# Attention scores of two heads issued together, with the low-part products on the two halves of the array

## What is computed

```python
def stick_breaking_attention(q, k, v):
    """q, k, v: (B, H, S, Dh). A[t,s] = beta_ts * prod_{s<j<t}(1 - beta_tj), strictly causal."""
    for start in range(0, S, SB_BLOCK):          # SB_BLOCK = 128 queries
        end = start + SB_BLOCK
        z = jnp.einsum('bhqd,bhkd->bhqk', qb, kb) * scale
        log_keep = jnp.where(valid, jax.nn.log_sigmoid(-z), 0.0)
        later = lax.cumsum(log_keep, axis=3, reverse=True) - log_keep
        w = jnp.where(valid, jnp.exp(jax.nn.log_sigmoid(z) + later), 0.0)
        outs.append(jnp.einsum('bhqk,bhkd->bhqd', w, vb))
```

## Time and profile before

| | |
|---|---|
| runs of before | 958.69 us median, 957.64 to 959.88 |
| profiled execution | 959.37 us, of it 957.4 us span |
| attention stage on PE | from 179.67 us (load of the first scores) to about 312 us |
| busy over the span | PE 932.1, PEld 783.3, DVE 515.2, ACT 325.8, POOL 215.9 us |
| granted PE clock | full but for a few short stretches |

### The profile page before, as it was taken

One profiled execution on the slowest core, in us unless ns is written; L12 is line 12 of the kernel. 1 busy time (PEld: TensorE's weight loads), 2 busy tenths in 40 slices (PEclk: granted clock), 3 DMA queues, 4 the chain that ended last, 5 costly groups with the idle time before them and its releaser, 6 DMA issues.

```text
span 957.4 us, 13833 instructions
## 1 busy us (share of the span) xinstructions
PE 932.1 (97%) x5547; PEld 783.3 (82%) x5547; DVE 515.2 (54%) x769; ACT 325.8 (34%) x740; POOL 215.9 (23%) x130
## 2 busy tenths in 40 slices
PE   6999999999999999999999999999999899999998
PEld 6788889778877888888888888888888678888886
DVE  4976899698986355444043183133336753334322
ACT  7852122487876221212811100223224720120000
POOL 0003414520010122222243222101110236762000
PEclk9999999999999999999999999999999999999999
DMA  9942503510211211111222536211117574435321
GB/s 315 296 146 71 150 2 110 157 35 25 58 48 42 66 52 44 44 44 56 78 77 90 153 100 172 83 45 55 46 51 251 185 240 106 153 115 180 106 88 66
DMA packets 122697, 100.55 MB, mean 105 GB/s; under 512 B 18087, under 2 KB 104704, under 8 KB 122378
## 3 DMA queue, kind: packets, MB, share of 16 engines
q1 hardware_dynamic: 92330, 76.07, 26.4%
q10 hardware_dynamic: 30304, 23.60, 8.1%
HBM read 73.44 MB, written 24.12 MB: 102 GB/s over the span
## 4 chain that ended last, share of the span: by engine, by line
PE 80%; DVE 11%; ACT 3%; DMA 2%; issue 2%; POOL 0%; SPq 0%; POOLq 0%; ACTq 0%; DVEq 0%
PE psum L845 48%; PE psum L272 5%; PE psum L274 5%; PE psum L273 5%; PE psum L281 4%; PE psum L1093 3%; DVE gacc L544 2%; DVE sq L720 2%; PE psum L1062 2%; PE psum L1430 1%; DMA adag<-in_ada_w 1%; PE psum L1064 1%; DVE ss L722 1%; DVE rows L732 1%; PE psum L1524 1%
## 5 line engine op out<-in xcount | busy, mean ns | idle before, releaser
L845 PE MATMUL psum<-hhi,w3hl 128*128 128x512 f32 x1120 | 368.3, 398 | 5.3 <-POOL w3hl L834 3.3
L845 PEld LDWEIGHTS psum<-hhi,w3hl 128*128 128x128 f32 x1120 | 211.0, 188 | 49.8 <-issue 6.5
L845 PE MATMUL psum<-hlo,w3hl 128*128 128x512 f32 x560 | 219.0, 391 | 0.0
L834 POOL TENSOR_TENSOR w3hl<-w3raw,w3hl 128x1024 fp32r<-128x1024 f32 x43 | 104.8, 2436 | 456.5 <-DVE w3hl L827 456.5
L845 PEld LDWEIGHTS psum<-hlo,w3hl 128*128 128x128 f32 x560 | 105.7, 189 | 19.7
L1192 DVE TENSOR_TENSOR_SCAN stick<-stick,floor 128x1024 f32<-128x1024 f32 (+7 forms) x64 | 89.3, 1441 | 14.4 <-ACT stick L1140 14.1
L845 PE MATMUL psum<-ohi,w3hl 128*128 128x512 f32 x256 | 79.0, 389 | 0.0
L929 ACT COPY zst<-psum 128x512 f32<-128x512 f32 x44 | 25.9, 588 | 131.4 <-PE psum L845 128.0
L680 PE MATMUL psum<-w,hhi 128*128 128x512 f32 x192 | 67.7, 397 | 0.6 <-ACT rows L704 0.6
L827 DVE CAST w3hl<-w3raw 128x1024 fp32r<-128x1024 f32 x43 | 29.5, 686 | 66.6 <-DMA w3raw<-in_w_in 36.7
L845 PEld LDWEIGHTS psum<-ohi,w3hl 128*128 128x128 f32 x256 | 48.0, 188 | 9.9
(11 more groups left out here) (228 smaller groups left out, 1556.2 us busy)
## 6 DMA issues: line engine op xcount, KB each, us to landing
z_scratch<-zst ACTq DMA_DIRECT2D x44, 256.0 KB, 2.3
w3raw<-in_w_in ACTq DMA_DIRECT2D x20, 512.0 KB, 4.2
ada<-in_ada_w SPq DMA_DIRECT2D x16, 512.0 KB, 7.5
w3raw<-in_w_in SPq DMA_DIRECT2D x16, 512.0 KB, 4.0
sg<-z_scratch SPq DMA_DIRECT2D x8, 1024.0 KB, 7.3
xrow<-in_x SPq DMA_DIRECT2D x4, 1024.0 KB, 6.1
w1raw<-in_w_in SPq DMA_DIRECT2D x4, 1024.0 KB, 7.1
adag<-in_ada_w SPq DMA_DIRECT2D x8, 512.0 KB, 4.0
```

Of the source, the lines that this page charges most:

```text
L834: nc.gpsimd.tensor_tensor(lo, w3raw[:], cast(hi), ALU.subtract).then_inc(w3_lo, 1)
L845: t = nc.tensor.matmul(out_, a[:, kt, :], moving[b][:, kt, 512 * half:512 * half + 512], start=(ends[0] and kt == k0 and m == 0), stop=(en ...
```

## The change

- `scores` runs at even steps only and makes the scores of both heads (steps n and n + 1): first the 128-row products of head 0 and head 1 (L1064 of the changed file), then the products with the keys' low parts (L1069), each over 64 rows: head 0 on partitions 0 to 63, head 1 on 64 to 127, the heads alternating, each into its own bank.
- Its wait on `keep_ok` is now for n, that is for the sigmoids of steps n - 2 and n - 1. At the first step of a pair it waits for all four `low` parts and all duplicates, where before the fourth `low` part was awaited by the second head alone.
- The high part of head 1 and the low parts are stored on the head's own partitions (`own_rows`); the duplicate of the keys goes out as two DMAs of 64x512 instead of one of 64x2x512.
- The zeros in `qk` part 2 and their two memsets on POOL, with the waits on them, are gone.

```diff
--- before.py
+++ after.py
@@ -994,6 +994,10 @@
         def o_cols(m):
             return bank(7)[:, P * (m % 2):P * (m % 2) + P]
 
+        def own_rows(head):
+
+            return slice(HD * head, HD * head + HD)
+
         def half_of(u):
 
             part, half = TURNS[u % 4]
@@ -1005,7 +1009,9 @@
 
                 pp, _, cols = half_of(u)
                 sp.wait_ge(fh_ok, u + 1)
-                sp.dma_start(cast(qk[HD:P, pp, 1, :, cols]), cast(qk[0:HD, pp, 1, :, cols])).then_inc(dup_ok, 16)
+                for head in range(2):
+                    a, b = own_rows(head), own_rows(1 - head)
+                    sp.dma_start(cast(qk[b, pp, 1, head, cols]), cast(qk[a, pp, 1, head, cols])).then_inc(dup_ok, 16)
 
             for u in range(2):
                 second_half(u)
@@ -1045,25 +1051,27 @@
                 f.then_inc(q_mm, 1)
 
             def scores(n):
-                pair, qb, head = steps[n]
-                if n == PER:
-                    pe.wait_ge(c2_ok, 3)
+
+                pair, qb, _ = steps[n]
                 if n % PER == 0:
-                    pe.wait_ge(fl_ok, 4 * pair + 3)
-                    pe.wait_ge(dup_ok, 32 * (pair + 1))
-                if n % PER == 1:
                     pe.wait_ge(fl_ok, 4 * pair + 4)
+                    pe.wait_ge(dup_ok, 64 * (pair + 1))
                 if n >= 2:
-                    pe.wait_ge(keep_ok, n - 1)
-                q, k_hi, k_lo = (qk[:, pair % 2, i, head] for i in range(3))
-                for c0 in range(0, keys(n), 512):
-                    c1 = min(c0 + 512, keys(n))
-                    z = bank(2 * (n % 2) + c0 // 512)
-                    nc.tensor.matmul(z[:, 0:c1 - c0], q[:, P * qb:P * qb + P], k_hi[:, c0:c1], start=True,
-                                     stop=False, skip_group_check=True)
-                    m = nc.tensor.matmul(z[:, 0:c1 - c0], q[:, P * qb:P * qb + P], k_lo[:, c0:c1], start=False,
-                                         stop=True, skip_group_check=True)
-                m.then_inc(z_mm, 1)
+                    pe.wait_ge(keep_ok, n)
+                parts = [(c0, min(c0 + 512, keys(n))) for c0 in range(0, keys(n), 512)]
+                for head in range(2):
+                    for c0, c1 in parts:
+                        nc.tensor.matmul(bank(2 * head + c0 // 512)[:, 0:c1 - c0],
+                                         qk[:, pair % 2, 0, head, P * qb:P * qb + P],
+                                         qk[:, pair % 2, 1, head, c0:c1], start=True, stop=False, skip_group_check=True)
+                for c0, c1 in parts:
+                    for head in range(2):
+                        m = nc.tensor.matmul(bank(2 * head + c0 // 512)[:, 0:c1 - c0],
+                                             qk[own_rows(head), pair % 2, 0, head, P * qb:P * qb + P],
+                                             qk[own_rows(head), pair % 2, 2, head, c0:c1], start=False, stop=True,
+                                             skip_group_check=True)
+                        if c1 == keys(n):
+                            m.then_inc(z_mm, 1)
 
             def flips(n):
 
@@ -1101,9 +1109,7 @@
             for u in range(4):
                 turn(u)
             fill_2(pe, -1)
-            pe.wait_ge(c2_ok, 1)
             scores(0)
-            scores(1)
             for n in range(NST + 5):
                 if n == 2:
                     pe.wait_ge(e_in, 16)
@@ -1111,7 +1117,7 @@
                         t = nc.tensor.transpose(bank(7)[:, ST * pair:ST * pair + ST], vE[:, P * pair:P * pair + P],
                                                 ident[0:ST, 0:ST])
                     t.then_inc(ve_mm, 1)
-                if n + 2 < NST:
+                if n % 2 == 0 and n + 2 < NST:
                     scores(n + 2)
                 fill_2(pe, n)
                 if turn_at(n) is not None:
@@ -1130,7 +1136,7 @@
                 if u == 4:
                     act.wait_ge(dv_ok, PAIRS)
                 for head in range(2):
-                    t = nc.scalar.copy(qk[0:HD, pp, part, head, cols], turn_bank(u)[HD * head:HD * head + HD])
+                    t = nc.scalar.copy(qk[own_rows(head), pp, part, head, cols], turn_bank(u)[own_rows(head)])
                 t.then_inc(fh_ok, 1)
 
             def keep(n):
@@ -1181,9 +1187,9 @@
                 pp, part, cols = half_of(u)
                 dve.wait_ge(fh_ok, u + 1)
                 for head in range(2):
-                    out_ = qk[0:HD, pp, 2, head, cols] if part else qk[HD:P, pp, 0, head, cols]
-                    t = nc.vector.tensor_tensor(out_, turn_bank(u)[HD * head:HD * head + HD],
-                                                cast(qk[0:HD, pp, part, head, cols]), ALU.subtract)
+                    a, b = own_rows(head), own_rows(1 - head)
+                    out_ = qk[a, pp, 2, head, cols] if part else qk[b, pp, 0, head, cols]
+                    t = nc.vector.tensor_tensor(out_, turn_bank(u)[a], cast(qk[a, pp, part, head, cols]), ALU.subtract)
                 t.then_inc(fl_ok, 1)
 
             def scan(n):
@@ -1195,7 +1201,7 @@
             for u in range(4):
                 low(u)
             dve.wait_ge(c2_in, 16)
-            dve.wait_ge(c2_ok, 2)
+            dve.wait_ge(c2_ok, 1)
             scan(0)
             for n in range(1, NST + 1):
                 if n < NST:
@@ -1210,19 +1216,13 @@
             split_hi(dve, T3 + 1)
 
         def pool_2(pool):
-            nc.gpsimd.memset(cast(qk[HD:P, 0, 2]), 0.0).then_inc(c2_ok, 1)
-            pool.wait_ge(c2_ok, 1)
             nc.gpsimd.memset(floor[:, 0:S - P], 0.0).then_inc(c2_ok, 1)
-            pool.wait_ge(c2_ok, 2)
             for pair in range(PAIRS):
                 if pair % 2 == 0:
                     pool.wait_ge(v_in[pair // 2], 16)
                 v = rows[:, 2, :, P * pair:P * pair + P]
                 nc.gpsimd.tensor_tensor(v, vsh[pair // 2][:, :, P * (pair % 2):P * (pair % 2) + P], v,
                                         ALU.subtract).then_inc(dv_ok, 1)
-            pool.wait_ge(dv_ok, PAIRS)
-            nc.gpsimd.memset(cast(qk[HD:P, 1, 2]), 0.0).then_inc(c2_ok, 1)
-            pool.wait_ge(c2_ok, 3)
             pool.wait_ge(q_mm, 8)
             split_lo(pool, 1)
             split_lo(pool, 2)
```

## The result

The changed kernel takes 997.57 us (median of six runs, 993.43 to 1001.53); the kernel before, on the same chip, 958.41 us (six runs, 955.37 to 959.88). The ratio is 1.0403, 95% interval 1.0385 to 1.0421: slower by 4.0%, or 39.2 us.

What follows compares the result with a forecast made beforehand. PE, 80% of the chain, was taken to bound the kernel. The terms 17.6 - 2.7 + 8.4 + 6.4 + 3.6 + 2.0 - 1.2 + 1.6 = 35.7 us gave 994 us, range 980 to 1008 us.

Steps and rivals of the forecast that it cites:

- Part 1: PE's even-step scores now also wait for the odd sigmoid: 30 waits, 17.6 us, with 2.7 us credited back.
- The hinge: At even steps both heads' scores use all four banks, so PE must wait for the preceding odd step's sigmoid.
- The credit of 2.7 us: ACT's sigmoids that were late only because their own scores were late now get them early: -2.7 us.
- Part 2: The block of scores on PE's path grows: +8.4 us if two heads' low products overlap, +16.8 us if serial.
- The rival of serial halves: Low products of the two row halves on PE do not overlap: +8.4 us on the sum, 1003 us; 15%.
- Part 3: PE's product shape changes to 64 rows and back, 0.20 us each: 6.4 us going in, 3.6 us out.
- Part 4: Start of the attention stage: scores(0) and scores(2) each +1.0 us, scores(3) with the first wait -1.2 us.
- Part 5: POOL's removed memsets, later duplicate DMAs, and ACT's and DVE's unchanged instructions were put at nothing.
- Part 6: One more fall of PE's granted clock in the attention stage, to the lower 1.2 GHz level: +1.6 us.
- The scans: DVE's scans bind at the heads of pairs two to four and hide the waits there: 983 us; 12%.
- The third: Short waits drop PE's clock in every second double step: 26 us in place of 1.6, 1019 us; 5%.
- The last two: PE alone decides the pace: 953 us with shape changes free, 3%; 959 us with them paid, 2%.

Runs made afterwards that it cites:

- Alone the wait: Kernel before, with even-step scores waiting for the sigmoids of both preceding steps, still one head at a time over 128 rows: 972.84 us.
- The copy_out pair: ACT's copy_out moved behind the second sigmoid, in the changed kernel (986.59 us) and, as control, in the kernel before (958.57 us).
- where they stood alone: Changed kernel's layout and 64-row low products, but each step makes its own head's scores with the waits of before: 971.19 us.
- the run with extra products: Changed kernel, with PE making head 0's first products once more ahead of its wait for the second sigmoid, all overwritten: 988.62 us.
- both heads over 128 rows: Kernel before, with both heads' scores issued at even steps, first products then low ones, all over 128 rows: 992.51 us.

## Why the prediction was right, point by point

The forecast was 994 us; measured are 997.57, inside the range, and on the side that had 0.95. Between the profiles the sum was 35.7 us, and 38.9 were found; the stage is 36.6 us longer, just above the 33 to 36 named. The mechanism is confirmed part by part, but the closeness of the total is in part luck: a wait priced too high stood against a clock priced too low.

*Part 1, the wait.* The hinge holds. Idle time before the loads of scores is 22.8 us in 26 waits, 0.9 us each, near the 30 of about 1 us that were named as the sign, and the double step went to 5.68 us, where 5.7 was named. Alone the wait is worth 14.8 us, 13.0 at full clock, under the 17.6 plus 1.0 for scores(2). A sum of 30 single differences does not see what one late step does to the next, and before, PE had 5.2 us of idle time in the stage that can take up part of it; which of these it was is not shown. The credit of 2.7 us is a small slip: 4.2 less 0.84 and 0.45 is 2.9. The copy_out pair is the best evidence that it is the ring.

*Part 2, the longer block.* The halves run side by side, 0.23 us for a pair of 512 columns, as the bound from below had it. The estimate after the Trainium skill (TensorE: Matmul & The Clock Gate, section Measured speedup vs the span model), a gain of 1.54 for two, would give 0.30 us for such a pair; the 0.23 us between the two timelines above speak against it for two halves of 64 rows. The rival of serial halves falls in the same place; made by force it takes 1009.8 us.

*Part 3, the changes of shape.* In the timeline 0.20 us each, as priced. The block of 512 keys above has two more rows to read, and one of 1024 keys shows two low pairs in a row:

```profile
285.13 0.40 PE L1064 MATMUL psum<-qk 128*128 128x512 f32 x1
...
286.23 0.40 PE L845 MATMUL psum<-hlo,rowsr 128*128 128x512 f32 x1
```

```profile
264.22 0.50 PE L1069 MATMUL psum<-qk 64*128 64x512 f32 x2
264.55 0.40 PE L1069 MATMUL psum<-qk 64*128 64x512 f32 x2
```

A product of 512 columns costs 0.23 us. From the last product over 128 rows (285.13) to the first low one (285.46) it is 0.33, so that one starts 0.10 late. And the first pair in the new shape holds PE for 0.33 (264.22 to 264.55), 0.10 longer than one product that follows its own shape. On the way out it is the same: 285.46 to 285.89 is 0.43, of it 0.33 for such a pair and 0.10 late, and then 0.34 to 286.23. So a change costs 0.10 us ahead of the first product and 0.10 in it, in either direction. In sum the changes came out cheap where they stood alone, 13.1 us for 64 of them in and some 50 out. The trace has 20 blocks, not 18, that are followed by products of 128 columns.

*Part 4, the start.* The load of scores(0) after:

```profile
179.08 0.76 PEld L1064 LDWEIGHTS psum<-qk 128*128 128x128 f32 x4 [1.66 <-DVE qk L1192]
```

PE waits 1.66 us for the low part, where the earlier trace rows had 0.66 of another kind: the +1.0 is there. What the prediction left at nothing is the same wait for the fourth low part at the heads of the other pairs. In the list of waits only one of these four is the start:

```profile
PEld psum L1064 <- DVE qk L1192: 4.3, 4, 1.7
```

The other three are 2.6 us together; before, there were 0.2 us of this wait in the stage. At the start, however, the projections ahead had ended 1.6 us earlier than in the profile before (last load 177.23 and 178.82), so the scores start 0.6 us earlier all the same. Why they had is not explained by the change.

*Part 5.* Right: POOL has no share in the chain, and DVE and ACT are as busy as before to within 2 us.

*Part 6, the clock.* This is the term that was mis-sized. "I count one more such fall, +1.6 us"; there are six more, some 10 us at full weight. The mean granted clock says the same: 0.986 of 996.3 us leaves 13.9 us, 0.995 of 957.4 leaves 4.8, so 9.1 us more; over all runs the estimate has 10.2. That the total was still near is owed to part 1. Without the clock the sum was 34.1 us, and 29.8 were found between the profiles, 4.3 less, while the clock came out 7.5 higher than its 1.6. The excess is in the wait: with the move of scores(2) it was priced at 18.6 us and gives 13.0 at full clock, while all other terms, 15.5 without the clock, come to 16.1 (981.0 less 964.9).

*The rivals.* The scans do not hide the waits: DVE's idle time before them rose from 14.4 to 44.4 us. The third, the clock that falls again and again, is half true: seven stretches in 32 double steps, not one in every second. What the Trainium skill describes (TensorE: Matmul & The Clock Gate, section A second HAM failure mode), a clock that swings under short pauses between groups of products, is what these windows show, and the run with extra products shows its price, 9.0 us. It should have been a term of the sum with a range of its own, and not a rival with 5%. The last two, in which PE alone decides, needed keep(n-1) earlier by what stands ahead of it in ACT's list; even with copy_out behind and the wait split it was 976.90.

The difference of 5.1 us between the change and both heads over 128 rows is mostly clock: by the estimate 3.9 us, and 1.3 for the rest, near the 1.6 that 10.0 for shapes less 8.4 for the stream had made. What is left open is whether those two are each of the size priced, since only their difference was measured, and how much of each fall of the clock lands on a wait.

## What to carry to other kernels

Two users that alternate on a double-buffered resource hide each other; serving both in one call takes all buffers at once and closes a ring over every engine in it, so price such a change by the chain of one round (here the late sigmoid), not by busy times, and expect a new order of one engine's list to hand the wait to the next scarce buffer. What stands in the ring ahead of the awaited instruction costs its whole time, and outside of the ring nothing (32 instructions of 0.26 us: some 7 us against none): look there first. Add to every new idle gap of PE what it may cost in clock, and before reading a difference between two runs compare their granted clocks.

## What the runs showed of the hardware that I had not expected

- Short idle times were enough to bring the clock down: no wait of PE for a sigmoid in the stage is longer than 2.5 us, and seven stretches of 3.4 us stand at 0.50.
- The runs of the change differ mostly by the clock: six of them spread over 8.1 us in span, and over 2.8 us in span times granted clock. For the kernel before, whose clock falls less, it is 5.8 and 4.6 us in 34 runs.
- Redundant products made a kernel faster, by 9.0 us for 46 of them.
- Two products that write the same PSUM partitions, in different banks, from two row halves cost no more than one (0.43 us with a change out of the shape, against 0.66).
- A change of shape costs as much into 64 rows as out of them, 0.20 us: the next product starts 0.10 us late (285.46, 285.89), and takes 0.10 us longer than one behind its own shape (264.22 to 264.55, 285.89 to 286.23, against 0.23).
